# Storing rounded rows and remainders of 256-token operands side by side, so that a 512-column product reads one run

## The chip, the cores and the metric

The kernel runs on one core of one Trainium2 chip. The metric is the device time of one execution in microseconds (us), as the median of several runs.

## What is computed

The reference is a chain of two small models over the same activations, all in float32. The first block puts 16 learned rows in front of 256 tokens of width 2048 and so works on 272 rows: a layer with latent attention, a gated feed-forward layer (5632 hidden columns), a layer with a gated linear recurrence, and a second feed-forward layer. The second block works on the 256 tokens alone: one layer that mixes grouped attention and differential attention, and one layer with dilated window attention. Almost all of the arithmetic is matrix products of the activations with weights:

```
first_block:   h = h + mla_mixer(rms_norm(h)) ; h = h + swiglu(rms_norm(h))          # 272 rows
               h = h + rglru_mixer(rms_norm(h)) ; h = h + swiglu(rms_norm(h))        # the last swiglu is needed for 256 rows only
second_block:  h = h + (attention_even(u @ w_in_even) * silu(gate)) @ w_out_even     # 256 rows
               h = h + (attention_odd(u @ w_in_odd) * silu(gate)) @ w_out_odd
               return rms_norm(h)
swiglu(h):     g, u = split(h @ w_gu) ; return (silu(g) * u) @ w_down
```

## The kernel before

Activations lie transposed: a column tile of 128 features is the partition axis and the tokens are the free axis. `X` holds the normed input of a layer, `H` its hidden values, each with 16 column tiles, and each value twice: as a rounded number ("fp32r") and as the remainder to the float32 value. `XH`/`XL` and `HH`/`HL` are the views of rounded and remainder. In the kernel before, one column tile k takes 2 x 272 elements of a partition: 272 rounded ones, then 272 remainders (`X2`, `H2`, lines 897 and 898). Weights arrive from HBM in units of 128 x 2048 elements (1 MB, three buffers). ScalarE rounds each unit into `WHt` (L1341), VectorE makes the remainder `WLt` (L1668).

A product with full accuracy is the sum of three: rounded weights x rounded rows, rounded weights x remainders, remainder of the weights x rounded rows. A group of the plan accumulates four output tiles in four PSUM banks over 16 column tiles, 4 of them per unit (`unit`, lines 1066 to 1117). For each k and each output tile there are three kinds:

- "rows": three products of 256 or 272 columns (L1105, L1106, L1107).
- "wide", for 256 tokens: one product of 512 columns that reads rounded rows and remainders together (L1096), and one of 256 columns with the remainder of the weights (L1097). The operand of the first is `X2[:, k, :, 16:272]`, which is two runs of 256 elements, 272 elements apart from start to start.
- "values": the activations are the stationary operand and the weights stream (L1100 to L1102).

The order of the groups is written out in `make_plan`: first feed-forward on 272 rows with "rows"; the recurrence layer with 272 rows for one half and "wide" tiles for its gate half; from the output product of the recurrence on (unit 205 of 501) everything is on 256 tokens. Each engine runs the plan's steps in order. The operands of the 256-token part are written by ScalarE (rounded) and VectorE (remainder) in pairs: `prepare` and `low_rows` for `X`; `gu_out`, `product` and `emit` for `H`.

Of the kernel before, what the change touches and what calls it, by code (L numbers as in the profile page):

```python
# [88 lines left out]
class Plan:  # L89
# [41 lines left out]

    def group(self, kunits, tiles, src, k0=0, fresh=None):
        g = len(self.groups)
        for i in range(len(tiles)):
            self.take("g", g, i)
        n0 = self.unit
        self.groups.append((n0, kunits, tiles, src, k0, fresh))
        for ku in range(kunits):
            n = n0 + ku
            self.of_unit[n] = (g, ku)  # L140
            self.step("unit", n)
            for block, fn in self.within.pop(n, []):
                at = len(self.steps)
                fn()
                self.inner[n, block] = self.steps[at:]
                self.moved.update(range(at, len(self.steps)))
            if ku < kunits - 1:
                self.mark("unit", "unit", n)
                self.end(n)
# [39 lines left out]
def make_plan():  # L189
# [191 lines left out]
    def out_proj(kunits, t0, fresh, stage, finish=(), scaled=False):  # L381
        for m in range(4):
            g = p.group(kunits, REG if not t0 else REGM if finish else WIDE, "H", 0, fresh if m == 0 else None)
# [46 lines left out]
    def ffn(l, t0, stage, finish, R):  # L430
# [3 lines left out]
        for pi, (f0, nf) in enumerate(PARTS):  # L434
            for j in range(f0 // 2, (f0 + nf) // 2):
                g = p.group(4, WIDE if t0 else REG, "X", 0, stage if j == 0 else None)
# [12 lines left out]
                p.close()  # L449
# [211 lines left out]
    stage_ = ["e"]  # L661
    g = p.group(4, REGM[:2] + VT, "X", 0, "ln_even")
    p.close()
# [24 lines left out]
    for q in range(4):  # L688
        g = p.group(4, REGM[0:2] + WIDE[2:4], "X")
        p.close()  # L690
# [87 lines left out]
    def pair_products(name, sides, fresh=None):  # L778
        odd = name[0] == "C"
        g = p.group(4, WIDE if odd else REGM, "X", 0, fresh)  # L780
        p.close()
# [6 lines left out]
        for i in range(4):  # L788
            if i in sides:
                p.after(i, sides[i])  # L790
        g = p.group(4, VT + WIDE[0:2], "X")
        p.close()
# [64 lines left out]
def build_program(nc, A, out):  # L857
# [8 lines left out]
    with ExitStack() as ctx:  # L866
# [30 lines left out]
        X2, H2 = (t[:, :].rearrange("p (k s n) -> p k s n", k=KD, s=2) for t in (Xt, Ht))  # L897
        XH, XL, HH, HL = X2[:, :, 0, :], X2[:, :, 1, :], H2[:, :, 0, :], H2[:, :, 1, :]
        ident, ones = cst[:, 0:128], cst[:, 128:256]
        R, RKV, RF, DG = (Rt[:, i * T:(i + 1) * T] for i in range(4))  # L900
# [158 lines left out]
        def _(t):  # L1059
# [6 lines left out]
            def unit(n):  # L1066
                g, ku = plan.of_unit[n]
                n0, kunits, tiles, src, k0, fresh = plan.groups[g]
                _, _, nk, ncol = SEQ[n]
                base = (n % NW) * U  # L1070
                xh, xl = (XH, XL) if src == "X" else (HH, HL)
                order = [(k, ti) for k in range(nk) for ti in range(len(tiles))]
                if n in plan.by_tile:
                    order = sorted(order, key=lambda o: o[1])
                for k, ti in order:
# [3 lines left out]
                    for c0, wd, t0, tn, kind in (tiles[ti],):  # L1079
# [10 lines left out]
                        wh, wl = WHt[:, w0:w0 + wd], WLt[:, w0:w0 + wd]  # L1090
                        ah, al = xh[:, k0 + kk, t0:t0 + tn], xl[:, k0 + kk, t0:t0 + tn]
                        first, last = kk == 0, ku == kunits - 1 and k == nk - 1
                        if kind == "wide":
                            o = two(bank[:, :])
                            both = (X2 if src == "X" else H2)[:, k0 + kk, :, t0:T]
                            t.matmul(o, wh, both, start=first, stop=False)  # L1096
                            m = t.matmul(o[:, 0, :], wl, ah, start=False, stop=last)  # L1097
# [236 lines left out]
        def _(a):  # L1334
# [24 lines left out]
            def prepare(stage, gain, mt, xfree, t0):  # L1359
                a.wait_ge(*when("r", stage, mt))  # L1360
                if mt == 0:
                    a.wait_ge(*when(*xfree))
                    if gain[0] == "gfe":
                        a.wait_ge(*when("gfe"))
                a.activation(XH[:, mt, t0:T], h[:, mt, t0:T], ACT.Identity, scale=gain_of(gain)).then_inc(sems["xh"], 1)

# [95 lines left out]
            def gu_out(l, j, g, k, turn, before, down, t0, r):  # L1462
# [5 lines left out]
                if down:  # L1468
                    a.wait_ge(*when(*down))
                a.activation(HH[:, k:k + 2, t0:T], u, ACT.Copy).then_inc(sems["hh"], 1)  # L1470

# [25 lines left out]
            def product(q, free):  # L1497
# [3 lines left out]
                if q == 0:  # L1501
                    a.wait_ge(*when(*free))
                a.activation(HH[:, 2 * q:2 * q + 2, M0:T], hs[:, :, M0:T], ACT.Copy).then_inc(sems["yh"], 1)

# [64 lines left out]
            def emit(hd, ready, hfree):  # L1569
                o = OT[:, 256 * (hd[1] % 2):256 * (hd[1] % 2) + 256]  # L1570
                a.wait_ge(*when(*ready))
                a.wait_ge(*when(*hfree))
                a.activation(HH[:, hd[1], M0:T], o, ACT.Copy).then_inc(sems["oh"], 1)

# [82 lines left out]
        def _(v):  # L1657
# [12 lines left out]
            def low_rows(k, gain, t0):  # L1670
                v.scalar_tensor_tensor(XL[:, k, t0:T], h[:, k, t0:T], gain, XH[:, k, t0:T].bitcast(f32),
                                       mult, sub).then_inc(sems["xl"], 1)
# [224 lines left out]
            def gu_out(l, j, g, k, turn, before, down, t0, r):  # L1897
# [14 lines left out]
                v.wait_ge(*when("hh", l, j))  # L1912
                v.tensor_tensor(HL[:, k:k + 2, t0:T], u, HH[:, k:k + 2, t0:T].bitcast(f32), sub).then_inc(sems["hl"], 1)

# [56 lines left out]
            def product(q, free):  # L1971
# [3 lines left out]
                v.wait_ge(*when("yh", q))  # L1975
                v.tensor_tensor(HL[:, 2 * q:2 * q + 2, M0:T], hs[:, :, M0:T], HH[:, 2 * q:2 * q + 2, M0:T].bitcast(f32),
                                sub).then_inc(sems["yl"], 1)
# [177 lines left out]
            def emit(hd, ready, hfree):  # L2155
                o = OT[:, 256 * (hd[1] % 2):256 * (hd[1] % 2) + 256]
                v.wait_ge(*when("oh", hd))
                v.tensor_tensor(HL[:, hd[1], M0:T], o, HH[:, hd[1], M0:T].bitcast(f32), sub).then_inc(sems["ol"], 1)

# [284 lines left out]
```

## Time and profile before

| | us |
|---|---|
| median of 3 runs | 3077.13 (3076.66 to 3077.99) |
| span of the profiled execution | 3075.5 |
| TensorE busy | 3057.3 |
| VectorE busy | 1841.4 |
| ScalarE busy | 1446.8 |
| GpSimd busy | 108.9 |
| read from HBM | 529 MB, 173 GB/s over the span |

The profile gives one execution. A matmul's row has its start and a modelled end, and the row of a product overlaps that of the next, so that the price of a product is read from start to start and not from its duration.

### The profile page before, as it was taken

How to read it: one execution, taken by the hardware profiler on the slowest of the kernel's cores; microseconds unless marked ns; L12 is line 12 of the kernel's file. 1: busy time of each engine (PE TensorE's matmuls, PEld its weight loads, DVE VectorE, ACT ScalarE, POOL GpSimd, SP SyncE). 2: the span in 40 equal slices, each digit the busy share in tenths (PEclk: the TensorE clock that was granted, in tenths of full speed). 3: DMA queues.
4: the chain of work that ended last, by engine and by line, in shares of the span. 5: the costliest groups of instructions: out<-in, count | busy, mean ns of one | idle time of the engine just before them, and what ended most of it. 6: DMA issues, size and time to landing. Idle time of an engine off the chain costs nothing.

```text
span 3075.5 us, 50379 instructions
## 1 busy us (share of the span) xinstructions
PE 3057.3 (99%) x22018; PEld 2887.6 (94%) x22018; DVE 1841.4 (60%) x2224; ACT 1446.8 (47%) x1660; POOL 108.9 (4%) x127
## 2 busy tenths in 40 slices
PE   9999999999999999999999999999999999999998
PEld 9889999999999999999888888889999999999998
DVE  7765555444445567765565655555786665656664
ACT  5544433333333457755443443446555554544543
POOL 0001000000000011110000000002000000000000
PEclk9999999999999999999999999999999999999999
DMA  6234545555545554455555455554444445444453
GB/s 237 105 104 170 174 174 176 177 178 178 175 168 180 177 185 177 156 206 180 190 192 191 179 193 191 189 187 172 179 144 158 175 169 192 165 168 175 165 178 124
DMA packets 78044, 534.46 MB, mean 174 GB/s; under 512 B 8576, under 2 KB 11136, under 8 KB 15104
## 3 DMA queue, kind: packets, MB, share of 16 engines
q1 hardware_dynamic: 77680, 531.10, 48.6%
q8 instruction: 173, 2.83, 0.4%
q14 instruction: 47, 0.39, 0.0%
q10 hardware_dynamic: 144, 0.15, 0.0%
HBM read 529.11 MB, written 2.10 MB: 173 GB/s over the span
## 4 chain that ended last, share of the span: by engine, by line
PE 97%; DVE 1%; ACT 1%; DMA 1%; issue 0%; SPq 0%; DVEq 0%; ACTq 0%
PE PB L1096 23%; PE PB L1106 17%; PE PB L1105 17%; PE PB L1107 17%; PE PB L1097 12%; PE PB L1100 2%; PE PB L1101 2%; PE PB L1102 2%; PE PB L1169 1%; DMA raw<-in_mla_in 1%; PE PB L1236 0%; PE PB L1257 0%; PE PB L1237 0%; DVE WLt L1668 0%; PE PB L1209 0%
## 5 line engine op out<-in xcount | busy, mean ns | idle before, releaser
L1668 DVE TENSOR_TENSOR WLt<-raw,WHt 128x2048 fp32r<-128x2048 f32 (+2 forms) x506 | 1140.3, 2260 | 802.2 <-ACT WHt L1341 801.6
L1341 ACT ACTIVATE WHt<-raw 128x2048 fp32r<-128x2048 f32 (+2 forms) x506 | 955.9, 1890 | 1161.8 <-PE PB L1107 562.6
L1096 PE MATMUL PB<-Xt,WHt 128*128 128x512 f32 x2624 | 935.6, 394 | 0.0
L1097 PE MATMUL PB<-Xt,WLt 128*128 128x256 f32 x2624 | 736.5, 281 | 0.0
L1105 PE MATMUL PB<-Xt,WHt 128*128 128x272 f32 (+1 forms) x2448 | 708.7, 289 | 2.9 <-ACT S L1479 1.3
L1106 PE MATMUL PB<-Xt,WHt 128*128 128x272 f32 (+1 forms) x2448 | 702.1, 287 | 0.0
L1107 PE MATMUL PB<-Xt,WLt 128*128 128x272 f32 (+1 forms) x2448 | 698.6, 285 | 0.0
L1096 PEld LDWEIGHTS PB<-Xt,WHt 128*128 128x128 f32 x2624 | 492.5, 188 | 97.6
L1106 PE MATMUL PB<-Ht,WHt 128*128 128x272 f32 (+1 forms) x1920 | 547.6, 285 | 0.0
L1105 PE MATMUL PB<-Ht,WHt 128*128 128x272 f32 (+1 forms) x1920 | 546.9, 285 | 0.2 <-DVE Ht L1840 0.2
L1107 PE MATMUL PB<-Ht,WLt 128*128 128x272 f32 (+1 forms) x1920 | 544.5, 284 | 0.0
L1097 PEld LDWEIGHTS PB<-Xt,WLt 128*128 128x128 f32 x2624 | 495.3, 189 | 0.0
L1105 PEld LDWEIGHTS PB<-Xt,WHt 128*128 128x128 f32 x2448 | 461.0, 188 | 12.6 <-DVE WLt L1668 3.0
L1106 PEld LDWEIGHTS PB<-Xt,WHt 128*128 128x128 f32 x2448 | 461.4, 188 | 1.4 <-issue 0.5
L1107 PEld LDWEIGHTS PB<-Xt,WLt 128*128 128x128 f32 x2448 | 460.6, 188 | 0.0
L1105 PEld LDWEIGHTS PB<-Ht,WHt 128*128 128x128 f32 x1920 | 362.0, 189 | 0.6 <-DVE Ht L1840 0.4
L1106 PEld LDWEIGHTS PB<-Ht,WHt 128*128 128x128 f32 x1920 | 361.6, 188 | 0.0
L1107 PEld LDWEIGHTS PB<-Ht,WLt 128*128 128x128 f32 x1920 | 361.7, 188 | 0.0
L2309 POOL TENSOR_TENSOR acct<-acct,sqt 128x256 f32<-128x256 f32 (+1 forms) x105 | 81.5, 784 | 2751.3 <-ACT sqt L1384 2743.5
L1096 PE MATMUL PB<-Ht,WHt 128*128 128x512 f32 x512 | 178.9, 393 | 0.0
L1100 PE MATMUL PB<-WHt,Xt 128*128 128x256 f32 (+1 forms) x512 | 147.9, 289 | 0.0
L1101 PE MATMUL PB<-WHt,Xt 128*128 128x256 f32 (+1 forms) x512 | 144.2, 282 | 0.0
(237 smaller groups left out, 2445.1 us busy)
## 6 DMA issues: line engine op xcount, KB each, us to landing
raw<-in_gu SPq DMA_DIRECT2D x176, 1024.0 KB, 4.7
raw<-in_dn SPq DMA_DIRECT2D x88, 1024.0 KB, 4.8
raw<-in_odd_in SPq DMA_DIRECT2D x64, 1024.0 KB, 4.7
raw<-in_even_in SPq DMA_DIRECT2D x52, 1024.0 KB, 4.8
raw<-in_lru_in SPq DMA_DIRECT2D x24, 1024.0 KB, 4.7
raw<-in_mla_o SPq DMA_DIRECT2D x16, 1024.0 KB, 4.7
raw<-in_lru_o SPq DMA_DIRECT2D x16, 1024.0 KB, 4.8
raw<-in_even_o SPq DMA_DIRECT2D x16, 1024.0 KB, 4.7
```

The lines of the kernel that those rows point to most:

```text
L1096: t.matmul(o, wh, both, start=first, stop=False)
L1097: m = t.matmul(o[:, 0, :], wl, ah, start=False, stop=last)
L1100: t.matmul(o, ah, wh, start=first, stop=False)
L1101: t.matmul(o, al, wh, start=False, stop=False)
L1102: m = t.matmul(o, ah, wl, start=False, stop=last)
L1105: t.matmul(o, wh, ah, start=first, stop=False)
L1106: t.matmul(o, wh, al, start=False, stop=False)
L1107: m = t.matmul(o, wl, ah, start=False, stop=last)
L1169: m = t.matmul(bank[0:q1 - q0, c0:c0 + k1], qn[:, q0:q1], kn[:, 0:k1], start=False, stop=c0 == 144)
L1341: a.activation(hi, r, ACT.Copy).then_inc(s_hi, 1)
L1668: v.tensor_tensor(lo, r, hi.bitcast(f32), sub).then_inc(s_lo, 1)
L2309: g.tensor_tensor(dst, dst, x, add).then_inc(sems["acc"], 1)
```

## The change

From the output product of the recurrence layer on, except in the groups that still need the old layout, operands of 256 tokens are stored and read with a second pair of views of the same two buffers. Column tile k then takes 512 elements: 256 rounded ones, then 256 remainders directly behind them, from element 16 of the buffer on. A "wide" product reads these 512 elements as one run, and its output is written as one run as well (it was one run before, named as two halves). "Rows" and "values" products of the same groups read their 256 or 128 elements from the new places. A flag `dense` on each group says which layout its operand has. The instructions that write operands have the same counts and sizes, with new addresses. Groups that keep the old layout are all those before unit 205: the 272-row groups, the "wide" tiles of the recurrence layer, and its last "rows" group on 256 tokens. No wait is added, removed or moved, and the order of the instructions is the same on each engine.

```diff
+        Xd, Hd = (t[:, 16:16 + 2 * KD * NT].rearrange("p (k m) -> p k m", k=KD) for t in (Xt, Ht))
+        DXH, DXL, DHH, DHL = Xd[:, :, 0:NT], Xd[:, :, NT:2 * NT], Hd[:, :, 0:NT], Hd[:, :, NT:2 * NT]
+
+        def x_rows(t0):
+            return (DXH, DXL) if t0 else (XH, XL)
...
-                xh, xl = (XH, XL) if src == "X" else (HH, HL)
+                xh, xl = (x_rows if src == "X" else h_rows)(dense)
...
-                        ah, al = xh[:, k0 + kk, t0:t0 + tn], xl[:, k0 + kk, t0:t0 + tn]
+                        r0 = t0 - M0 if dense else t0
+                        ah, al = xh[:, k0 + kk, r0:r0 + tn], xl[:, k0 + kk, r0:r0 + tn]
...
                             o = two(bank[:, :])
-                            both = (X2 if src == "X" else H2)[:, k0 + kk, :, t0:T]
-                            t.matmul(o, wh, both, start=first, stop=False)
+                            if dense:
+                                t.matmul(bank[:, :], wh, (Xd if src == "X" else Hd)[:, k0 + kk, :], start=first, stop=False)
+                            else:
+                                both = (X2 if src == "X" else H2)[:, k0 + kk, :, t0:T]
+                                t.matmul(o, wh, both, start=first, stop=False)
                             m = t.matmul(o[:, 0, :], wl, ah, start=False, stop=last)
...
-                a.activation(XH[:, mt, t0:T], h[:, mt, t0:T], ACT.Identity, scale=gain_of(gain)).then_inc(sems["xh"], 1)
+                a.activation(x_rows(t0)[0][:, mt, :], h[:, mt, t0:T], ACT.Identity, scale=gain_of(gain)).then_inc(sems["xh"], 1)
...
-                a.activation(HH[:, k:k + 2, t0:T], u, ACT.Copy).then_inc(sems["hh"], 1)
+                a.activation(h_rows(t0)[0][:, k:k + 2, :], u, ACT.Copy).then_inc(sems["hh"], 1)
...
-                a.activation(HH[:, hd[1], M0:T], o, ACT.Copy).then_inc(sems["oh"], 1)
+                a.activation(DHH[:, hd[1], :], o, ACT.Copy).then_inc(sems["oh"], 1)
```

The writers of the remainders on VectorE (`low_rows`, `gu_out`, `product`, `emit`) and the writer `product` on ScalarE are changed in the same way.

## Rows read from the trace of the kernel before

**Rows 1.** The page: busy time and share of each engine; TensorE's clock in 40 slices.
```profile
PE 3057.3 (99%) x22018; PEld 2887.6 (94%) x22018; DVE 1841.4 (60%) x2224; ACT 1446.8 (47%) x1660; POOL 108.9 (4%) x127
...
PEclk9999999999999999999999999999999999999999
```
**Rows 2.** The chain that ended last, by engine, then by line.
```profile
PE 97%; DVE 1%; ACT 1%; DMA 1%; issue 0%; SPq 0%; DVEq 0%; ACTq 0%
PE PB L1096 23%; PE PB L1106 17%; PE PB L1105 17%; PE PB L1107 17%; PE PB L1097 12%; PE PB L1100 2%; PE PB L1101 2%; PE PB L1102 2%; PE PB L1169 1%; DMA raw<-in_mla_in 1%; PE PB L1236 0%; PE PB L1257 0%; PE PB L1237 0%; DVE WLt L1668 0%; PE PB L1209 0%
```
**Rows 3.** Busy time by stretch: us, then busy (x count) per engine, clock, DMA share, GB/s.
```profile
1312.20:1403.50 91.30, 91.30 (x771) 91.30 (x770) 54.90 (x56) 46.03 (x50) 11.61 (x13) 1.00 0.53 193
...
1403.50:2142.80 739.30, 739.30 (x4421) 656.74 (x4420) 428.75 (x407) 329.34 (x312) 19.01 (x26) 1.00 0.52 188
...
2576.60:2967.70 391.10, 391.10 (x2523) 356.12 (x2522) 245.30 (x294) 195.76 (x248) 2.95 (x4) 1.00 0.49 172
```
**Rows 4.** Groups of instructions, shapes apart: line, shape, xcount | busy us, mean ns.
```profile
L1096 PE MATMUL PB<-Xt,WHt 128*128 128x512 f32 x2624 | 935.6, 394 | 0.0
L1105 PE MATMUL PB<-Ht,WHt 128*128 128x256 f32 x960 | 270.8, 282 | 0.0
L1096 PE MATMUL PB<-Ht,WHt 128*128 128x512 f32 x512 | 178.9, 393 | 0.0
L1105 PE MATMUL PB<-Xt,WHt 128*128 128x256 f32 x480 | 138.8, 289 | 1.8 <-ACT S L1479 1.3 <-DVE WLt L1668 0.4
```
**Rows 5.** The same view of the recurrence layer alone, 1107.3 to 1312.2 us.
```profile
L1096 PE MATMUL PB<-Xt,WHt 128*128 128x512 f32 x192 | 72.0, 397 | 0.0
L1105 PE MATMUL PB<-Xt,WHt 128*128 128x256 f32 x64 | 18.6, 290 | 1.8 <-ACT S L1479 1.3 <-DVE WLt L1668 0.4
```
**Rows 6.** TensorE in order of time, start and duration in us, "wide" units 241 to 248.
```profile
1515.65 0.39 PE L1096 MATMUL PB<-Xt,WHt 128*128 128x512 f32 x1
...
1517.05 0.40 PE L1096 MATMUL PB<-Xt,WHt 128*128 128x512 f32 x1
...
1518.44 0.39 PE L1096 MATMUL PB<-Xt,WHt 128*128 128x512 f32 x1
...
1519.85 0.40 PE L1096 MATMUL PB<-Xt,WHt 128*128 128x512 f32 x1
...
1560.34 0.39 PE L1096 MATMUL PB<-Xt,WHt 128*128 128x512 f32 x1
```
**Rows 7.** TensorE in order of time, "rows" units 205 to 208, 256 columns.
```profile
1312.17 0.28 PE L1105 MATMUL PB<-Ht,WHt 128*128 128x256 f32 x1
...
1313.61 0.28 PE L1105 MATMUL PB<-Ht,WHt 128*128 128x256 f32 x1
...
1315.02 0.28 PE L1105 MATMUL PB<-Ht,WHt 128*128 128x256 f32 x1
...
1334.99 0.28 PE L1105 MATMUL PB<-Ht,WHt 128*128 128x256 f32 x1
```
**Rows 8.** TensorE in order of time, "rows" units 69 to 72, 272 columns.
```profile
484.65 0.29 PE L1105 MATMUL PB<-Xt,WHt 128*128 128x272 f32 x1
...
508.60 0.29 PE L1105 MATMUL PB<-Ht,WHt 128*128 128x272 f32 x1
```
**Rows 9.** The 512-column products of L1222: durations ns min/median/max, then both merged, in time.
```profile
L1222 PE MATMUL PB<-S,cst x2: 592/592/593, 2179.5 to 2180.0; 128*128 128x512 f32 x2
...
2179.52 1.02 PE L1222 MATMUL PB<-S,cst 128*128 128x512 f32 x2
```
**Rows 10.** TensorE's waits, longest first: us in total, times, longest.
```profile
PE PB L1149 <- DVE Rt L1739: 2.5, 1, 2.5
```
**Rows 11.** Weight preparation in the second feed-forward layer; DMA issues with us to landing.
```profile
L1668 DVE TENSOR_TENSOR WLt<-raw,WHt 128x2048 fp32r<-128x2048 f32 x132 | 300.3, 2290 | 269.4 <-ACT WHt L1341 269.4
...
L1341 ACT ACTIVATE WHt<-raw 128x2048 fp32r<-128x2048 f32 x132 | 252.3, 1913 | 292.0 <-PE PB L1097 282.8 <-PE PB L1107 9.0
...
raw<-in_gu SPq DMA_DIRECT2D x176, 1024.0 KB, 4.7
```

More of the change, by code:

```diff
@@ L130, in inside, with group @@
         self.within.setdefault(self.unit + k, []).append((block, fn))
-    def group(self, kunits, tiles, src, k0=0, fresh=None):
+    def group(self, kunits, tiles, src, k0=0, fresh=None, dense=False):
         g = len(self.groups)
@@ L136, in group @@
         n0 = self.unit
-        self.groups.append((n0, kunits, tiles, src, k0, fresh))
+        self.groups.append((n0, kunits, tiles, src, k0, fresh, dense))
         for ku in range(kunits):
@@ L382, in out_proj @@
         for m in range(4):
-            g = p.group(kunits, REG if not t0 else REGM if finish else WIDE, "H", 0, fresh if m == 0 else None)
+            g = p.group(kunits, REG if not t0 else REGM if finish else WIDE, "H", 0, fresh if m == 0 else None, bool(t0))
             for i in range(4):
@@ L435, in ffn @@
             for j in range(f0 // 2, (f0 + nf) // 2):
-                g = p.group(4, WIDE if t0 else REG, "X", 0, stage if j == 0 else None)
+                g = p.group(4, WIDE if t0 else REG, "X", 0, stage if j == 0 else None, bool(t0))
                 for i in range(4):
@@ L661, in make_plan @@
     stage_ = ["e"]
-    g = p.group(4, REGM[:2] + VT, "X", 0, "ln_even")
+    g = p.group(4, REGM[:2] + VT, "X", 0, "ln_even", True)
     p.close()
@@ L688, in make_plan @@
     for q in range(4):
-        g = p.group(4, REGM[0:2] + WIDE[2:4], "X")
+        g = p.group(4, REGM[0:2] + WIDE[2:4], "X", dense=True)
         p.close()
@@ L779, in pair_products @@
         odd = name[0] == "C"
-        g = p.group(4, WIDE if odd else REGM, "X", 0, fresh)
+        g = p.group(4, WIDE if odd else REGM, "X", 0, fresh, True)
         p.close()
@@ L790, in pair_products @@
                 p.after(i, sides[i])
-        g = p.group(4, VT + WIDE[0:2], "X")
+        g = p.group(4, VT + WIDE[0:2], "X", dense=True)
         p.close()
@@ L898, in build_program, with h_rows @@
         XH, XL, HH, HL = X2[:, :, 0, :], X2[:, :, 1, :], H2[:, :, 0, :], H2[:, :, 1, :]
+        Xd, Hd = (t[:, 16:16 + 2 * KD * NT].rearrange("p (k m) -> p k m", k=KD) for t in (Xt, Ht))
+        DXH, DXL, DHH, DHL = Xd[:, :, 0:NT], Xd[:, :, NT:2 * NT], Hd[:, :, 0:NT], Hd[:, :, NT:2 * NT]
+        def x_rows(t0):
+            return (DXH, DXL) if t0 else (XH, XL)
+        def h_rows(t0):
+            return (DHH, DHL) if t0 else (HH, HL)
         ident, ones = cst[:, 0:128], cst[:, 128:256]
@@ L1067, in unit @@
                 g, ku = plan.of_unit[n]
-                n0, kunits, tiles, src, k0, fresh = plan.groups[g]
+                n0, kunits, tiles, src, k0, fresh, dense = plan.groups[g]
                 _, _, nk, ncol = SEQ[n]
                 base = (n % NW) * U
-                xh, xl = (XH, XL) if src == "X" else (HH, HL)
+                xh, xl = (x_rows if src == "X" else h_rows)(dense)
                 order = [(k, ti) for k in range(nk) for ti in range(len(tiles))]
@@ L1502, in product @@
                     a.wait_ge(*when(*free))
-                a.activation(HH[:, 2 * q:2 * q + 2, M0:T], hs[:, :, M0:T], ACT.Copy).then_inc(sems["yh"], 1)
+                a.activation(DHH[:, 2 * q:2 * q + 2, :], hs[:, :, M0:T], ACT.Copy).then_inc(sems["yh"], 1)
             def head_in(name, b, i, g, gain, tfree, free):
@@ L1670, in low_rows @@
             def low_rows(k, gain, t0):
-                v.scalar_tensor_tensor(XL[:, k, t0:T], h[:, k, t0:T], gain, XH[:, k, t0:T].bitcast(f32),
+                xh, xl = x_rows(t0)
+                v.scalar_tensor_tensor(xl[:, k, :], h[:, k, t0:T], gain, xh[:, k, :].bitcast(f32),
                                        mult, sub).then_inc(sems["xl"], 1)
@@ L1912, in gu_out @@
                 v.wait_ge(*when("hh", l, j))
-                v.tensor_tensor(HL[:, k:k + 2, t0:T], u, HH[:, k:k + 2, t0:T].bitcast(f32), sub).then_inc(sems["hl"], 1)
+                hh, hl = h_rows(t0)
+                v.tensor_tensor(hl[:, k:k + 2, :], u, hh[:, k:k + 2, :].bitcast(f32), sub).then_inc(sems["hl"], 1)
             def lru_start(before):
@@ L1975, in product @@
                 v.wait_ge(*when("yh", q))
-                v.tensor_tensor(HL[:, 2 * q:2 * q + 2, M0:T], hs[:, :, M0:T], HH[:, 2 * q:2 * q + 2, M0:T].bitcast(f32),
+                v.tensor_tensor(DHL[:, 2 * q:2 * q + 2, :], hs[:, :, M0:T], DHH[:, 2 * q:2 * q + 2, :].bitcast(f32),
                                 sub).then_inc(sems["yl"], 1)
@@ L2157, in emit @@
                 v.wait_ge(*when("oh", hd))
-                v.tensor_tensor(HL[:, hd[1], M0:T], o, HH[:, hd[1], M0:T].bitcast(f32), sub).then_inc(sems["ol"], 1)
+                v.tensor_tensor(DHL[:, hd[1], :], o, DHH[:, hd[1], :].bitcast(f32), sub).then_inc(sems["ol"], 1)
             def last_gain(mt):
```

## The prediction

> **What bounds the kernel now.** I first read the busy shares of the page: TensorE is at 99% of the span, VectorE at 60%, ScalarE at 47%, and the clock line shows full speed in every slice [rows 1]. A busy share alone says little about TensorE, since rows of matmuls overlap, so I went to the chain that ended last: 97% of it is TensorE, and L1096, the product that is edited, has the largest single share with 23% [rows 2]. Then the stretches. In those where the new layout applies and "wide" products dominate, TensorE is busy for the whole stretch at granted clock 1.00 (the 2.4 GHz level), while VectorE is busy 58% and ScalarE 45% of the second feed-forward layer (428.8 and 329.3 of 739.3 us), and DMA engines about half [rows 3]. TensorE's longest wait anywhere is 2.5 us, once, in the tail [rows 10]. So the time from 1312 us on is the number of products times their distance from start to start, and only a change of that distance moves the end.
>
> **What the change touches, counted.** There are 2624 + 512 = 3136 wide products of 512 columns [rows 4]. The 192 of the recurrence layer keep the old layout [rows 5], so 2944 get the one-run operand. Of the "rows" products with 256 columns there are 960 + 480 triples [rows 4], of which 64 keep the old layout [rows 5]: 1376 triples, 4128 products, read the same 256 elements from another address.
>
> **The price of a product, from start to start.** The view in order of time gives starts to 0.01 us, so I take long stretches without a wait.
> - Wide: units 241 to 248 are 8 x 16 = 128 pairs (512 columns, then 256). From 1515.65 to 1560.34 us are 44.69 us, 349.1 ns a pair [rows 6].
> - 256 columns: units 205 to 208 are 4 x 48 = 192 products, 22.82 us, 118.9 ns each [rows 7].
> - 272 columns: 192 products in 23.95 us, 124.7 ns each [rows 8].
>
> At 2.4 GHz, with a column per cycle, 256 columns are 106.7 ns and 272 are 113.3 ns. What stays is 12.2 ns at 256 and 11.4 ns at 272: a fixed part that does not grow with the columns, as far as 16 columns can show. The 512-column product is the pair less one 256-column product: 349.1 - 118.9 = 230.2 ns, against 213.3 ns for its columns. What stays is 16.9 ns, which is 4.7 ns more than at 256 and 5.5 ns more than at 272. The two-run operand is the one thing by which this product differs from the others apart from its length.
>
> The Trainium skill ("TensorE: Matmul & The Clock Gate", Back-to-back issue gap) gives a warm distance of N/2.4 plus about 2.5 ns with no term that grows with N. The trace agrees in form at 256 and 272 columns, not in size (11.4 to 12.2 ns), and departs from it at the two-run 512. By that page's figure the fixed part would be far smaller and a one-run product would take 215.8 ns; the sum here does not use it.
>
> **The terms of the sum.**
> 1. Removed: the break between the two runs in 2944 products. Its cost shows in no row by itself. Upper bound: the whole excess over the dearer reading, 5.5 ns, or 2944 x 5.5 = 16.2 us. Lower bound: nothing, if the excess belongs to the length and not to the break. I take 4.7 ns, because the fixed part at 256 comes from a stretch of the same 256-token part: 2944 x 4.7 = 13.8 us. For the upper bound speaks also that the only warm products with 512 columns in one run start 1.02 - 0.59 = 0.43 us apart (float32 operands, not rounded ones; two cycles a column at 2.4 GHz are 426.7 ns) and so carry a fixed part of only about 3 ns [rows 9]: length alone does not have to bring an extra. That is one pair of products of another type, so it is weak.
> 2. Moved addresses. In the old layout a column tile is 2176 bytes long, in the new one 2048, so that all operand starts lie at the same distance from a multiple of 256 bytes, where even and odd k differ by 128 bytes today. The rows show a difference between even and odd k: four wide pairs take 1.40 and 1.41 us at even k and 1.39 us at odd k [rows 6]; twelve 256-column products take 1.44 and 1.41 us [rows 7]. Whether operand address or weight address (which alternates by 2048 bytes from k to k and keeps doing so) makes it, the rows do not say. If all blocks ran like one or the other parity, wide pairs would change by half of 0.015 us / 4, that is 1.9 ns, or 2944 x 1.9 = 5.6 us, and the 256-column products by half of 0.03 us / 12, 1.25 ns, or 4128 x 1.25 = 5.2 us. Bounds: -10.8 to +10.8 us. I take 0, the middle, since nothing shows which parity the new address will resemble.
> 3. Writers of the operands. ScalarE and VectorE issue the same instructions with the same sizes at other places, also with the inner runs of 256 they have now: 0. They lie under TensorE; if one of them took 10% longer, at 45 and 58% busy it would stay under it [rows 3].
> 4. Waits, DMAs, queues: none is added, removed or moved, and reload order on the queue of SyncE is the same: 0.
> 5. What is late next, if TensorE gets faster? A wide unit is 16 pairs, 5.59 us, and would be 5.51 us. For each unit ScalarE spends 1.91 us on rounding, VectorE 2.29 us on the remainder, and 1 MB lands 4.7 us after its issue, with three buffers [rows 11]. The idle time before L1341 ends at TensorE's release of a weight buffer (282.8 of 292.0 us), so the producers wait for TensorE and not it for them. They have room for 0.08 us more speed per unit.
>
> Sum: -13.8 us, all of it on the path. The span goes from 3075.5 to 3061.7 us. The median of the runs lies 1.6 us above the span, which stays, so 3077.1 - 13.8 = 3063.3 us.
>
> **Rivals.**
> - *No change.* The excess belongs to the length. If the cost above the columns' own time grows with them (some stall per kilobyte read), the line from 118.9 ns at 256 to 230.2 ns at 512 is 0.435 ns a column against 0.417, and one run of 512 sits on that line too. Then the time stays at 3077, with term 2 around it. Against it: this line asks for 125.9 ns at 272 columns, and the stretch gives 124.7 [rows 8], below even the 125.5 of a fixed part. For it: 16 columns are a short lever, and the excess would be just as large. The Trainium skill ("Advanced Engine Details and Errata", Memory Cachelines) puts the cost at crossing 16-byte lines with fewer than two hits, and both layouts touch the same number of such lines, so that by it the gain is 0 and the time 3077 us; no row here has crossings of that kind to test it. That the edit does nothing is this case too: 512 columns a product in both kernels, the same count. Chance 0.36.
> - *Slower: every block takes the dearer parity.* The new layout puts all k at one phase. If that phase is the one of the dear blocks and the break costs nothing, term 2 comes in full: 3077.1 + 10.8 = 3087.9 us. It decides for "slower" when its share reaches 6.2 of 10.8 us, that is when about 79% of the blocks take the dear pattern instead of half. For it: term 2's difference between blocks is regular in the stretches. Against it: it needs both a free break and the wrong phase, and the weight address may be the cause instead. Chance 0.12.
> - *The break costs something, but not all of the excess*: 1 to 2 ns of it, 3 to 6 us, 3071 to 3074. It lies between the forecast and "no change", and I count it half to each.
>
> **How the numbers follow.** A difference of 0.2%, 6.2 us, is about what a measurement of this kernel can tell from no change. Forecast with its part of the last rival: 0.52; no change within 0.2% with the other part: 0.36; slower: 0.12. The likeliest case alone reaches from 3077.1 - 16.2 - 5 = 3056 to 3077.1 - 13.8 + 6 = 3069 us (half of term 2 on either side). The range has to take in "no change" with half of term 2 above it: 3077.1 + 5.4 = 3082.5, rounded to 3083. Outside remain the upper part of the slower rival and a gain in full of both terms, together under 0.2.
>
> **What would show it.** In the changed kernel the shape at what was L1096 is still 128x512, 2944 of them on one line and 192 on the other. If the forecast is right, 16 pairs of a wide unit take 5.51 us in place of 5.59, everywhere in the dense part, and the 256- and 272-column units keep their times. The 192 that keep two runs stay at their distance, beside the others in the same trace. If the pair stays at 349 ns, the excess is the length's. If the alternation between even and odd k vanishes, term 2 hangs on the operand's address, and its sign is read from the 256-column units, 5.71 us for four k today. The prediction would be wrong as a whole if TensorE began to wait for weights, which would show as idle time before the first product of a unit.

## The result, and the profile after

The changed kernel takes 3082.19 us (median of 20 runs, 3081.85 to 3083.13), the kernel before 3077.14 us in the same runs: ratio 1.0017, 95% interval 1.0011 to 1.0023. The forecast was 3063.3 us. The change costs 5 us where 14 us of gain were expected, and it stays just under the 0.2% that I had called distinguishable; with 20 runs it is told apart all the same.

The page of the changed kernel, against [rows 1, 2]: shares and clock as before, the chain still 97% TensorE. The edited product is now L1105, and L1108 is what is left with two runs.

```profile
span 3080.1 us, 50379 instructions
...
PE 3062.7 (99%) x22018; PEld 2893.5 (94%) x22018; DVE 1841.7 (60%) x2224; ACT 1447.0 (47%) x1660; POOL 109.0 (4%) x127
...
PE 97%; DVE 1%; ACT 1%; DMA 1%; issue 0%; SPq 0%; DVEq 0%; ACTq 0%
```

The groups by shape: 2432 + 512 products with one run, and, in the recurrence layer, 192 with two. Their durations are modelled and show nothing (393 to 397 ns in both kernels). Against [rows 4, 5]:

```profile
L1105 PE MATMUL PB<-Xt,WHt 128*128 128x512 f32 x2432 | 864.9, 393 | 0.0
L1105 PE MATMUL PB<-Ht,WHt 128*128 128x512 f32 x512 | 179.9, 393 | 0.0
```
```profile
L1108 PE MATMUL PB<-Xt,WHt 128*128 128x512 f32 x192 | 72.0, 397 | 0.0
```

TensorE's waits, against [rows 10]: the same 2.5 us, nothing new.

```profile
PE PB L1161 <- DVE Rt L1752: 2.5, 1, 2.5
```

So again only starts tell. TensorE in order of time, units 241 to 248, against [rows 6]; the last row is the first product of unit 249:

```profile
1516.79 0.40 PE L1105 MATMUL PB<-Xt,WHt 128*128 128x512 f32 x1
1517.03 0.28 PE L1109 MATMUL PB<-Xt,WLt 128*128 128x256 f32 x1
1517.15 0.40 PE L1105 MATMUL PB<-Xt,WHt 128*128 128x512 f32 x1
1517.38 0.28 PE L1109 MATMUL PB<-Xt,WLt 128*128 128x256 f32 x1
1517.50 0.39 PE L1105 MATMUL PB<-Xt,WHt 128*128 128x512 f32 x1
1517.73 0.28 PE L1109 MATMUL PB<-Xt,WLt 128*128 128x256 f32 x1
...
1561.74 0.39 PE L1105 MATMUL PB<-Xt,WHt 128*128 128x512 f32 x1
```

44.95 us for 128 pairs are 351.2 ns a pair, 2.0 more than the 349.1 before. And the 256-column units 205 to 208, against [rows 7]: 23.04 us for 192 products, 120.0 ns in place of 118.9.

```profile
1311.86 0.28 PE L1117 MATMUL PB<-Ht,WHt 128*128 128x256 f32 x1
...
1334.90 0.28 PE L1117 MATMUL PB<-Ht,WHt 128*128 128x256 f32 x1
```

That is not so in all 60 of these units. In the kernel before, nearly every one of them without other work in it takes 5.707 us. In the new kernel the first 28 take 5.760 us, but most of the 32 of the two attention layers take 5.69 to 5.70 us, slightly less than before. Units 409 to 412 take 22.78 us, 118.6 ns a product:

```profile
2512.73 0.28 PE L1117 MATMUL PB<-Ht,WHt 128*128 128x256 f32 x1
...
2535.51 0.28 PE L1117 MATMUL PB<-Ht,WHt 128*128 128x256 f32 x1
```

The 24 units of the recurrence layer that keep two runs take 150.8 us in both kernels. Summed over whole units (start of a unit's first product to that of the next), the 152 all-wide units take 4.4 us more than before, the 256-column units on `H` 1.3 us more, the units of values and wide tiles 0.9 us less, the rest 0.2 us less: 4.6 us, the difference of the two spans.

### The profile page after: what moved, and what is told of

It reads as the page before. It is cut to its first block, busy times and chain, and to the rows that moved or that the text cites. A ratio compares the mean times of both kernels' runs of the same rounds, so it can differ in the third digit from the quotient of the medians.

```text
span 3080.1 us, 50379 instructions
## 1 busy us (share of the span) xinstructions
PE 3062.7 (99%) x22018; PEld 2893.5 (94%) x22018; DVE 1841.7 (60%) x2224; ACT 1447.0 (47%) x1660; POOL 109.0 (4%) x127
## 4 chain that ended last, share of the span: by engine, by line
PE 97%; DVE 1%; ACT 1%; DMA 1%; issue 0%; SPq 0%; DVEq 0%; ACTq 0%
PE PB L1105 22%; PE PB L1118 17%; PE PB L1117 17%; PE PB L1119 17%; PE PB L1109 12%; PE PB L1112 2%; PE PB L1113 2%; PE PB L1114 2%; PE PB L1108 1%; PE PB L1181 1%; DMA raw<-in_mla_in 1%; PE PB L1248 0%; PE PB L1269 0%; PE PB L1249 0%; DVE WLt L1680 0%
## 5 line engine op out<-in xcount | busy, mean ns | idle before, releaser
L1105 PE MATMUL PB<-Xt,WHt 128*128 128x512 f32 x2432 | 864.9, 393 | 0.0
L1105 PEld LDWEIGHTS PB<-Xt,WHt 128*128 128x128 f32 x2432 | 457.0, 188 | 93.5
L1117 PEld LDWEIGHTS PB<-Xt,WHt 128*128 128x128 f32 x2448 | 461.1, 188 | 12.0 <-DVE WLt L1680 2.3
L1118 PEld LDWEIGHTS PB<-Xt,WHt 128*128 128x128 f32 x2448 | 461.6, 189 | 1.4 <-issue 0.5
L1105 PE MATMUL PB<-Ht,WHt 128*128 128x512 f32 x512 | 179.9, 393 | 0.0
L1112 PE MATMUL PB<-WHt,Xt 128*128 128x256 f32 (+1 forms) x512 | 148.0, 289 | 0.0
L1109 PE MATMUL PB<-Ht,WLt 128*128 128x256 f32 x512 | 144.8, 283 | 0.0
```

The source lines that it names most:

```text
L1105: t.matmul(bank[:, :], wh, (Xd if src == "X" else Hd)[:, k0 + kk, :], start=first, stop=False)
L1112: t.matmul(o, ah, wh, start=first, stop=False)
L1117: t.matmul(o, wh, ah, start=first, stop=False)
L1118: t.matmul(o, wh, al, start=False, stop=False)
```

## The experiments

Two views of the same question: whole kernels with one thing changed, timed against the kernel before on the same chip, and stand-alone kernels in which TensorE alone runs stretches of 64 groups, each on a line of its own, so that a stretch's price is the distance between the first products of two neighbouring stretches, divided by 64. Each of the four stand-alone kernels was executed once.

### Join and tile distance taken apart

The stand-alone loop, here for two runs; only start, tile distance and gap change from stretch to stretch:

```
for n in range(16):
    for i in range(4):
        wh, wl = w(n, i)                       # WHt / WLt at 512 * (n % 4) + 128 * i
        t.matmul(two(PB[i]), wh, runs(16 + 544 * n, 2, 16), start=n == 0, stop=False)
        m = t.matmul(PB[i][:, 0:256], wl, Xt[:, 16 + 544 * n:16 + 544 * n + 256], start=False, stop=n == 15)
```

> Leaves out the whole model: TensorE alone runs 26 stretches of 64 groups on one rounded buffer (16 column tiles x 4 output tiles), each stretch with another layout of the moving operand, weights changing as in the kernel; the output is no result of the model. Theory A (starts): what a product costs beyond its columns hangs on where its operand starts within a small block of bytes, not on whether it is one run. Then the pair of the old layout (tile 544, gap 16) repeats 349.1 ns and the new one (tile 512) 351.3 ns with nothing else running; one run at tile 544 lies near the old, two planes of 256 near the new, and the pairs shift with the start of the buffer by some ns. Theory B (the break costs 4.7 ns, and the denser tile costs 6.9 ns on top of it): one run at tile 544 takes 344.4 ns, two planes 356 ns, whatever the start. Theory C (other engines' traffic makes the difference): with TensorE alone both layouts take the same time, within 0.3 ns. 512 columns alone, without a 256-column product between: by B the two-run form is 4.7 ns dearer than the one-run form, by A the difference can have either sign.

First products of the first five stretches (old layout; new layout; one run at tile 544; two planes; one run at tile 512 from start 0):

```profile
29.38 0.39 PE L65 MATMUL PB<-Xt,WHt 128*128 128x512 f32 x1
51.73 0.39 PE L71 MATMUL PB<-Xt,WHt 128*128 128x512 f32 x1
74.18 0.40 PE L77 MATMUL PB<-Xt,WHt 128*128 128x512 f32 x1
96.68 0.39 PE L84 MATMUL PB<-Xt,WHt 128*128 128x512 f32 x1
119.15 0.39 PE L90 MATMUL PB<-Xt,WHt 128*128 128x512 f32 x1
```

Per pair: 22.35 / 64 = 349.2 ns, 350.8, 351.6, 351.1 ns. With nothing else running the kernel's two prices come back within 0.4 ns, so theory C falls: no other engine is needed for the difference. Two planes cost what one run costs, so the break costs nothing and theory B falls. The third stretch has the starts and the tile distance of the first and lacks only the gap of 16 elements between the runs: it costs 2.4 ns more, so where the second run lies does count. 512 columns without a product between took 232.3 ns in one run and 232.1 ns in two. One-run pairs from other starts took 353.2 (0), 350.2 (8), 353.1 (32) and 353.2 ns (48).

Stretches of the same kernel with one product at a time, in one run from start 16 at tile 512, tell what length alone costs. First products of the stretch and of the next, for 512, 256 and 384 columns:

```profile
299.48 0.39 PE L138 MATMUL PB<-Xt,WHt 128*128 128x512 f32 x1
314.35 0.40 PE L143 MATMUL PB<-Xt,WHt 128*128 128x512 f32 x1
```
```profile
389.92 0.28 PE L169 MATMUL PB<-Xt,WHt 128*128 128x256 f32 x1
397.60 0.28 PE L174 MATMUL PB<-Xt,WHt 128*128 128x256 f32 x1
...
413.18 0.34 PE L184 MATMUL PB<-Xt,WHt 128*128 128x384 f32 x1
424.44 0.22 PE L189 MATMUL PB<-Xt,WHt 128*128 128x128 f32 x1
```

They are 232.3, 120.0 and 175.9 ns a product: 0.44 ns a column from 256 to 384 and from 384 to 512, where a column per cycle of 2.4 GHz is 0.417. One run of 512 columns is thus 5.6 ns above the price of 256 columns plus 106.7 ns, without any break in it. This is the line of the rival "no change" (0.435 ns a column).

In the whole kernel, tile distance alone:

```diff
-        Xd, Hd = (t[:, 16:16 + 2 * KD * NT].rearrange("p (k m) -> p k m", k=KD) for t in (Xt, Ht))
+        Xd, Hd = (t[:, :].rearrange("p (k m) -> p k m", k=KD)[:, :, M0:M0 + 2 * NT] for t in (Xt, Ht))
```

> The new kernel with column tiles 544 elements apart as in the old one, rounded values and remainders still side by side (one run of 512, then 32 unused elements). Undoes the new tile distance alone. Theory A (starts of the operands): the wide pairs fall back to the old kernel's price, near 349 ns, the time to about 3077 us, give or take 4. Theory B (the break did cost, the new tile distance ate the gain): the wide pair takes about 344.4 ns, 2944 of them give 3077 - 14 = 3063 us. If neither the join nor the distance matters for what was seen: 3082 us as with the whole change.

Measured 3083.65 us, ratio 1.0021 (1.0011 to 1.0030). Neither forecast: the join with the old tile distance is no better, just as its stand-alone stretch says (351.6 ns). The run takes the change apart. Its wide units take 5.627 us, against 5.587 before and 5.620 with the whole change, so the dearer wide pair comes from closing the gap and not from the tile distance. Its 256-column units on `H` stay at the 5.707 us of the kernel before, so the 5.760 us of the new kernel come from the tile distance. And the join alone undone:

```diff
+        Xd, Hd = (t[:, 16:16 + 2 * KD * NT].rearrange("p (s k m) -> p k s m", k=KD, s=2) for t in (Xt, Ht))
+        DXH, DXL, DHH, DHL = Xd[:, :, 0, :], Xd[:, :, 1, :], Hd[:, :, 0, :], Hd[:, :, 1, :]
...
+                                t.matmul(o, wh, (Xd if src == "X" else Hd)[:, k0 + kk, :, :], start=first, stop=False)
```

> The new kernel with all rounded rows in one plane of the buffer and all remainders in a second one 4096 elements behind, column tiles 256 elements apart: the wide product reads two runs again, and every operand starts at the same distance from a multiple of 1024 bytes as in the new kernel. Undoes the join alone. Theory A: 256-column products take 120.0 ns as in the new kernel, wide pairs 351 ns, the time stays at 3082 us within 4. Theory B: the two runs cost 4.7 ns again on top: wide pairs 356 ns, 3082 + 14 = 3096 us.

Measured 3082.09 us (ratio 1.0016, 1.0007 to 1.0025) against 3082.19 with one run. 2944 products went back to two runs and nothing changed: the 152 all-wide units (2432 pairs) take 868.2 us in both traces, and units 241 to 248 take 44.95 us, as in the new kernel. The break is worth less than 0.1 ns a product.

```profile
1517.21 0.40 PE L1105 MATMUL PB<-Xt,WHt 128*128 128x512 f32 x1
...
1562.16 0.39 PE L1105 MATMUL PB<-Xt,WHt 128*128 128x512 f32 x1
```

### Prices by start

> Leaves out the whole model: TensorE alone runs 52 stretches of 64 groups as in m1_layouts, now with one thing moved at a time: the start of the moving operand in steps of 4 elements, the start of the weights, the gap between rounded values and remainders. Theory A (starts): with the same start for every product, 256 columns alone took 120.0 ns at start 16, and 117.5 ns as a mean of two starts at tile 544; so some starts cost less than 117.5 and others more than 120 ns, the price repeats when the start moves by 64 elements (start 80 costs what 16 costs), and wide pairs follow it with differences of several ns between starts. Theory D (mixture): what saves time is not a start but that starts alternate from product to product, so that any constant start costs 120.0 ns and 232.4 ns at 512 columns, whatever it is. Theory E (weights): moving the weights by 8 elements changes the price as much as moving the operand by 8, since the two reads meet; by theory A alone it changes nothing.

Prices in ns, from stretch to stretch, from all four stand-alone kernels (start in elements of 4 bytes; "-" was not measured):

```
start                  0      4      8      12     16     20     24     28
256 columns alone      117.8  119.8  119.9  113.7  118.6  118.7  117.3  119.2
512 columns alone      228.9    -    233.5    -    232.4    -    234.2    -
pair, one run          353.2  353.2  350.1  353.3  351.1  346.8  347.0  350.1
triple 256, tile 512   340.0* 355.1  359.9  341.1  355.8* 356.1  356.0* 357.7
triple 272, tile 544   374.2  378.3  375.2  374.6  376.6  372.9  375.7  375.3
                                      (* other values elsewhere, see below)
```

Theory D falls: constant starts differ by up to 6 ns a product. At the eight starts from 0 to 56 in steps of 8, one run of 512 costs 0.6 to 13.1 ns more than 256 columns plus 106.7 ns, 7.6 ns in the mean. Starts 80, 144 and 272 cost what 16 costs (118.6 to 118.7), so the price repeats with 64 elements; in the 272-column row, taken from the third stand-alone kernel, it repeats with 32 within 0.4 ns. Theory E holds: moving the weights changes the price. With 256 columns alone at start 16, weights shifted by 8, 16 and 32 give the prices of the starts at the same distance (119.9, 117.8 and 119.8 ns, as at 8, 0 and 48). Shifts of 4 and 48 do not: 119.9 and 117.8 ns, where starts 12 and 32 took 113.7 and 113.6.

Two starts in the whole kernel, by one number in the diff (`t[:, 16:16 + ...` to 0 or 24):

> The new kernel with its one-run layout starting at element 0 of the buffer in place of 16; nothing else differs. By the price list of the two stand-alone kernels: 2944 wide pairs at 353.4 ns in place of 351.2 (+6.5 us), 1376 triples of 256-column products at 340 ns in place of 360 (-27.5 us), against the new kernel's 3082.2: 3061 us. If the list's prices of stand-alone stretches don't carry over to the kernel (theory F: the price hangs on what ran before a stretch and not on its layout alone), the triples stay near 353 to 360 and the time comes out between 3080 and 3089 us. Theory B (only the join matters): unchanged 3082 us.

> The new kernel with its layout starting at element 24. By the price list: wide pairs 346.7 ns in place of 351.2 (2944 x -4.5 = -13.2 us), triples 356.0 in place of 360.0 (1376 x -4 = -5.5 us), so about 3063.5 us, which would be faster than both kernels; theory F: within 4 us of 3082; theory B: 3082 us.

Start 0: 3080.64 us (ratio 1.0011, 1.0001 to 1.0020), not 3061. Wide units took 5.655 us, 353.4 ns a pair, as listed, but 256-column units 5.653 us, 353.3 ns a triple and not 340. Start 24: 3069.79 us (ratio 0.9975, 0.9965 to 0.9985), faster than both kernels; from 1514.92 to 1559.29 us are 346.6 ns a pair, and the excess over 3063.5 lies in units of values and wide tiles (303.4 us in place of 301.5) and of rows on `X`, which had no price in the list.

```profile
1514.92 0.39 PE L1105 MATMUL PB<-Xt,WHt 128*128 128x512 f32 x1
...
1559.29 0.39 PE L1105 MATMUL PB<-Xt,WHt 128*128 128x512 f32 x1
```

> Leaves out the whole model: TensorE alone, 39 stretches, to see whether the price of a layout hangs on the stretch before it. 256 columns alone at start 16 took 120.0 ns in one kernel and 118.67 in the other: if the history counts (theory F), this kernel's repeats differ among themselves by 1 ns or more, and rows at start 0 after three different stretches too (340.0 once so far). If the layout alone counts, each repeat agrees within 0.1 ns: rows at start 0 340.0, rows at 24 356.0, wide at 24 and 56 346.7, wide at 16 351.2. New in it: 272-column triples at tile 544 from start 0 to 60; the kernel's cost 373 to 375 ns, and if one slot of 6.67 ns per product is the least that comes on top of the columns, the best start gives 360 ns.

History counts in places. The triple at start 0 in the second stand-alone kernel, then in the third (first products of the stretch and of the next; in the third, two such stretches with a wide one between):

```profile
584.38 0.28 PE L297 MATMUL PB<-Xt,WHt 128*128 128x256 f32 x1
606.14 0.28 PE L305 MATMUL PB<-Xt,WHt 128*128 128x256 f32 x1
```
```profile
51.64 0.28 PE L72 MATMUL PB<-Xt,WHt 128*128 128x256 f32 x1
74.25 0.39 PE L79 MATMUL PB<-Xt,WHt 128*128 128x512 f32 x1
96.44 0.28 PE L86 MATMUL PB<-Xt,WHt 128*128 128x256 f32 x1
119.05 0.40 PE L93 MATMUL PB<-Xt,WHt 128*128 128x256 f32 x2
```

21.76 / 64 = 340.0 ns, but 353.3 ns in the third, twice. One layout can settle in either of two patterns and keep it. It was seen at starts 0 and 32 (340.0 and 353.3), 24 (356.0 and 352.1) and 16 (355.8 and 360.0); wide pairs gave the same price at each repeat within 0.5 ns, and so did 272-column triples 32 elements on. Whole kernels show it too. With start 24, 24 of the 60 256-column units on `H` take 5.63 us (352 ns a triple) and most others about 5.70 (356). The 5.760 and 5.69 to 5.70 us of the new kernel are the two prices of start 16.

### Distance to the weights

> Leaves out the whole model: TensorE alone, 31 stretches. Question: does the price hang on the operand's start by itself, or on the distance between it and the start of the weights that are loaded at the same time? Theory G (distance): only the difference counts, in a period of 32 elements (128 bytes). Then one run at start 24 with weights shifted by 8 costs the 351.2 ns of start 16 with weights at 0, with weights shifted by 24 the 353.4 of start 0, start 16 with weights shifted by 8 the 350.0 of start 8, and the old layout at start 40 with weights shifted by 24 its own 349.15. Theory A (the operand's start alone): start 24 keeps 346.7 ns under every shift of the weights, start 16 keeps 351.2. Further, the old layout itself moved as a whole by 4 to 28 elements: by both theories its pair leaves 349.15 for most shifts, between 346.7 and 354 ns; if the old layout is insensitive, all eight stay within 0.3 ns.

First products of the stretches "one run, start 24" with weights shifted by 0, 8, 24 and 40, then of the next one:

```profile
592.91 0.40 PE L248 MATMUL PB<-Xt,WHt 128*128 128x512 f32 x1
615.11 0.40 PE L254 MATMUL PB<-Xt,WHt 128*128 128x512 f32 x1
637.58 0.40 PE L260 MATMUL PB<-Xt,WHt 128*128 128x512 f32 x1
660.19 0.40 PE L266 MATMUL PB<-Xt,WHt 128*128 128x512 f32 x1
682.38 0.40 PE L272 MATMUL PB<-Xt,WHt 128*128 128x512 f32 x1
```

346.9, 351.1, 353.3 and 346.7 ns. The second and third are the prices of starts 16 and 0 with weights in place, and the old layout at start 40 with weights shifted by 24 took 349.3 ns, the price of its start 16 and not the 351.4 of start 40. Start 16 with weights shifted by 8 gave 350.7, between start 8 (350.1 to 350.2) and start 16 (350.9 to 351.1), and decides nothing. The fourth does not fit: 351.1 was due by a period of 32, 353.2 by one of 64 (start 48), and it kept the price of its own start. So of five shifts three speak for distance, one against it, and one is undecided.

The old layout moved as a whole by 0 to 28 elements took 349.1, 348.5, 349.2, 348.7, 350.7, 350.7, 351.4 and 347.2 ns a pair. So I moved the operands of the kernel before, with a diff of one line:

```diff
         ht = hx[:, KD:KD + KD * T]
+        spare = sb("spare", 4)
```

> The kernel before, unchanged but for 4 unused elements allocated ahead of the operand buffers, so that X and H start 16 bytes further from the weights; layout, runs and instructions are the old ones. Theory G (the price is set by where operand and weights start relative to each other): from the stand-alone price list at a shift of 4: 3136 wide pairs at 348.3 in place of 349.2 (-2.7 us), 1440 triples of 256 columns at 355.0 in place of 356.7 (-2.4 us), 2928 triples of 272 columns at 378.4 in place of 374.2 (+12.2 us): 3077.2 + 7 = 3084 us, a larger move than the whole change made. If the old kernel's time does not hang on starts: 3077.2 us.

> The kernel before with 28 unused elements ahead of X and H in place of 4. Theory G with the list at a shift of 28: wide 346.65 (3136 x -2.5 = -7.9 us), 256-column triples 354.15 (-3.6 us), 272-column triples 375.0 (+2.4 us): 3077.2 - 9 = 3068 us, as fast as the one-run layout at start 24, with two runs. Else 3077.2 us.

Measured 3078.23 us (ratio 1.0003, 0.9994 to 1.0013) and 3079.23 us (1.0006, 0.9997 to 1.0016), neither 3084 nor 3068. The unit prices tell why: in the first, 256-column units take 22.67 us for four and 272-column units 24.00 us, which are 354.2 and 375.0 ns a triple, the list's prices for a shift of 8 and not of 4. In the second 356.7 and 374.2 ns are what a period of 32 gives for a shift of 32; its wide pair took 350.0 ns in place of 349.2, so for wide pairs that period does not hold. The prices fit an allocation that rounds a buffer up to 8 elements, so that 4 moved the operands by 8 and 28 by 32; the addresses themselves were not read.

```profile
485.61 0.28 PE L1106 MATMUL PB<-Xt,WHt 128*128 128x272 f32 x1
...
509.61 0.28 PE L1106 MATMUL PB<-Ht,WHt 128*128 128x272 f32 x1
...
1314.45 0.28 PE L1106 MATMUL PB<-Ht,WHt 128*128 128x256 f32 x1
...
1337.12 0.28 PE L1106 MATMUL PB<-Ht,WHt 128*128 128x256 f32 x1
```

The decisive run moves weights and operands of the kernel before together, by 8 elements, with `spare` ahead of `raw`:

> The kernel before with 8 unused elements ahead of everything, so that weights and operands move together by 32 bytes and keep their distance. Theory G (distance between operand and weights): every stretch costs what it does in the kernel before, 272-column units 5.987 us, 256-column units 5.707, wide units 5.587, time 3077.2. Theory A (the operand's own start): the prices of the run in which the operands alone moved by 8: 6.000, 5.667 and 5.587 us, time 3078.2.

Measured 3077.32 us (ratio 1.0001, 0.9992 to 1.0010). The same four places: 23.94 and 22.83 us, the prices of [rows 7, 8] and not the 24.00 and 22.67 above. For these two prices and this shift, the distance counts and not the place. The wide unit can't tell: it takes 5.587 us in the kernel before and in both of these runs.

```profile
484.84 0.29 PE L1106 MATMUL PB<-Xt,WHt 128*128 128x272 f32 x1
...
508.78 0.29 PE L1106 MATMUL PB<-Ht,WHt 128*128 128x272 f32 x1
...
1312.35 0.28 PE L1106 MATMUL PB<-Ht,WHt 128*128 128x256 f32 x1
...
1335.18 0.28 PE L1106 MATMUL PB<-Ht,WHt 128*128 128x256 f32 x1
```

### A kernel set by the list

> Two planes (two runs per wide product) with starts at element 24 in place of 16. If one run or two makes no difference at any start: wide units 5.547 us and 3069.8 us, as with one run at 24. If the equality at start 16 was chance, the wide unit differs from 5.547 us.

Measured 3069.42 us (ratio 0.9976, 0.9966 to 0.9985) against 3069.79 with one run: one run or two is the same at this start too.

> The new kernel with X starting at element 24 and H at element 12. Against the run with both at 24 (3069.8 us): 512 wide pairs of H at 353.3 in place of 346.7 (+3.4 us); 960 triples of H at 340 in place of 355.8 ns (-15.1 us) if the cheap state of start 12 carries over from the stand-alone stretches: 3058 us. At starts 0 and 32 the same stretch showed 340.0 in some places and 353.3 in others; if such a second state takes hold here, the triples cost 353 to 360 and the time is 3071 to 3077 us.

Measured 3061.20 us (ratio 0.9948, 0.9933 to 0.9963). The forecast with the cheap pattern was 3058. It holds in almost every 256-column unit on `H` without other work in it: 1312.01 to 1333.83 us are 21.82 us for 192 products, and four units of the second feed-forward layer fall out of it (5.59 to 5.74 us in place of 5.440). These 60 units gain 12.3 us and not 15.1, since 24 of them already ran in the cheaper pattern at start 24.

> As the one before, with 20 unused elements ahead of X and H and the starts inside the buffers set back, so that X keeps its place and H lies at 76 (12 and one period of 64); what moves is the old layout of the first half: 2928 triples of 272 columns from 374.2 to 372.5 ns (-5 us), the 192 wide pairs there +1.6 ns. Expected 5 us below the run before: 3053 us if its cheap state holds, 3066 to 3072 if not.

Measured 3084.82 us (ratio 1.0025, 1.0016 to 1.0034). By the same rounding the 20 elements had become 24, so that X lay at 28, H at 80 and the old layout at 24. Its units fit those places: 6.013 us for 272 columns (375.8 ns a triple; list 375.7), 5.620 us for wide on `H` (351.2, as at 16), 5.600 us for wide on `X` (350.0; list 350.1). For 4 elements it came out 24 us above the run before and 32 above its forecast.

The last kernel gives each use its own start inside the buffers and pads nothing ahead of them:

```diff
+        Xt, Ht = sb("Xt", 2 * KD * T + 64, f32r), sb("Ht", 2 * KD * T + 64, f32r)
...
+        X2, H2 = (t[:, 20:20 + 2 * KD * T].rearrange("p (k s n) -> p k s n", k=KD, s=2) for t in (Xt, Ht))
...
+        Xd, Hd, Hw = (t[:, at:at + 2 * KD * NT].rearrange("p (k m) -> p k m", k=KD) for t, at in ((Xt, 24), (Ht, 12), (Ht, 24)))
```

> One-run layout with a start for each use, from the price list: X at 24, H at 24 where wide products read it and at 12 where 256-column products do, the 272-row layout moved by 20 inside buffers 64 elements longer. Against the run with X at 24 and H at 12 (3061.2 us): 512 wide pairs back to 346.7 from 353.3 ns (-3.4 us), 2928 triples of 272 columns from 374.2 to 372.5 ns (-5.0 us), 192 old wide pairs and 64 old triples about +0.3 us: 3053 us.

Measured 3053.08 us (ratio 0.9923, 0.9906 to 0.9939), 24 us below the kernel before and 29 below the change, at the forecast. Its rows at the places of [rows 6 to 8], in order of time: 272 columns 23.83 us for four units, 256 columns 21.80 us (113.5 ns a product), wide 44.37 us (346.6 ns a pair).

```profile
483.74 0.29 PE L1118 MATMUL PB<-Xt,WHt 128*128 128x272 f32 x1
...
507.57 0.29 PE L1118 MATMUL PB<-Ht,WHt 128*128 128x272 f32 x1
...
1307.72 0.28 PE L1118 MATMUL PB<-Ht,WHt 128*128 128x256 f32 x1
...
1329.52 0.28 PE L1118 MATMUL PB<-Ht,WHt 128*128 128x256 f32 x1
...
1506.34 0.39 PE L1106 MATMUL PB<-Xt,WHt 128*128 128x512 f32 x1
...
1550.71 0.39 PE L1106 MATMUL PB<-Xt,WHt 128*128 128x512 f32 x1
```

## Why the prediction was wrong

- **What bounds the kernel**: right. TensorE's spacing of products is all that moved; the eleven variants of the whole kernel differ by up to 32 us with the same number of products, and no wait on TensorE grew beyond 2.5 us.
- **The counts** (2944, 192, 1376): right. The 416 triples of "values" that also read the new places were not counted; their units came out 0.9 us cheaper.
- **Term 1, the break at 4.7 ns**: this is the step that failed. I read a fixed part of 12.2 ns at 256 columns, found 16.9 at 512, and gave the difference to the one visible thing, the two runs. It is not the break: planes and one run agree to 0.1 us at start 16 and to 0.4 us at start 24. A product of 512 columns in one run carries the excess as well: at start 16 it costs 0.44 ns a column from 256 columns on, so that it stands 5.6 ns above 256 columns plus 106.7 ns. The excess goes with the length, and it varies with the start: 512 columns alone cost 227.1 to 234.2 ns, that is 13.8 to 20.9 ns over a column per cycle, and 256 alone 6.9 to 13.3. The fixed part is no constant; I subtracted the price of one layout and length from that of another. The 272-column stretch, which I took as evidence against a part that grows with length, was a third layout with a start of its own. The Trainium skill ("TensorE: Matmul & The Clock Gate", step-by-step) says that loading the next tile's weights does not steal read bandwidth from the running matmul; here moving the operands by 8 elements against the weights changes the price (356.7 to 354.2 ns a triple) and moving both does not. That the two reads disturb each other is my inference from it; no run counts their accesses.
- **Term 2, moved addresses, taken as 0 with bounds of 10.8 us either way**: the right thing with the wrong value. It was the whole effect. Per wide pair it was +2.0 ns against a bound of 1.9, per 256-column product +1.1 against 1.25 in 28 of the 60 units on `H`, and slightly below 0 in most of the others. The term had only the distance between column tiles in it; for the wide pairs that was not the cause. With the old tile distance and the gap closed they cost 351.7 ns, with the new one 351.2: what made them dearer is that the remainders moved 64 bytes nearer to the rounded rows. That the alternation between even and odd k vanishes (triples of the new kernel repeat at 360.0 ns, and wide pairs run in a cycle of three) shows that the operand's address was in it. The one term whose existence rows did show was set to 0, and the one that no row showed by itself carried 14 us.
- **Terms 3, 4 and 5**: right. ScalarE and VectorE changed by less than 0.4 us of busy time each.
- **The rivals**: "no change" gave 3077 with term 2 around it, and "slower" 3087.9 us; the result lies between. The first had the excess right, which belongs to the length and stays in one run. The 5 us come by the mechanism of the second (a free break, and starts that are dearer on the whole). Its trigger, one parity's price for all blocks, was too simple: start 16 is dear for wide pairs and for triples, slightly cheap for units of values and wide tiles.

Open is what makes the pattern: why the price repeats with 32 elements in some products and only with 64 in others, why three of ten shifts of the weights did not fit the distance, and what puts a stretch into one of two patterns. The runs give prices, not a mechanism inside the memory.

## What to carry to other kernels

When TensorE is busy throughout, price a layout change by where each operand starts relative to the weights loaded beside it, and measure that in a stand-alone kernel with a stretch for each start: its prices carried over to the whole kernel within 0.5 ns a product, except that a stretch with two patterns can come out in the other one (353.3 ns a triple where 340 was forecast). Before an excess in a row is given to the feature that catches the eye, measure a product without the feature: here one run of 512 had the same excess. Padding a buffer by a few elements may move it by another number than written, so set starts inside a buffer.

## What the runs showed of the hardware

- Two runs of 256 rounded float32 elements as moving operand, 16 KB apart, cost what one run of 512 does (3082.09 against 3082.19 us, 3069.42 against 3069.79 us, 2944 products each). With 64 bytes between the runs the pair cost 349.2 ns, against 351.6 for one run from the same start.
- Alone and in one run from start 16, products of 256, 384 and 512 columns cost 120.0, 175.9 and 232.3 ns, 0.44 ns a column.
- At granted clock 1.00 a 256-column product with weights of 128 columns cost 113.3 to 120 ns from start to start, changing with the starts of operand and weights in steps as small as 16 bytes. Over the whole kernel that range is worth at least 32 us, 1% (3053.08 to 3084.82 us).
- The same layout can hold one of two prices (340.0 and 353.3 ns a triple at start 0; 360.0 and 356 in two parts of the new kernel). What decides between them was not found.
